# Decay-gate logits before the softmax attention, two value products in its last units, and GLA outputs with tokens on partitions

## The chip, the cores and the metric

The kernel runs on one core of a Trainium2 chip. The metric is the device time of one execution in microseconds (us), smaller is better. A comparison of this kernel with another can tell about 0.3% (some 3 us) from no change.

## The reference

One layer of a streaming encoder for 512 prompt tokens and 32 sample tokens (544 in all), D = 1024, all in float32. Cut to what the change touches:

```
h  = rmsnorm(x)
cq, ckv, kpe, gq, gk, gv, glr, gr, ga, gb = split(h @ w_in)
o_a = softmax attention over 8 heads (chunk causal)
la  = log_sigmoid(glr @ w_gate2 + b_gate2) / 16          # the decay gates, 4 heads x 128
o_g, state = gla(gq, gk, gv, la, state0)                 # 4 heads, keys 128, values 256 wide
o_b = rmsnorm(o_g over the 256 values of a head) * g_gla_norm * silu(gr)
x  += ( sigmoid(ga) * (o_a @ w_a) + sigmoid(gb) * (o_b @ w_b) ) @ w_out
x  += mixture of 32 experts, 2 of them per token;  y = rmsnorm(x)
```

## The kernel before, in words

Activations stand with features on partitions and the 544 tokens along the free dimension. A projection tile ("product", e.g. `("gv", 3)`) makes 128 features for all tokens: the weight tile is loaded (SyncE queue), its high part cast on ScalarE (`high`), its low part subtracted on GpSimd (`split`), and TensorE adds three terms (high x high, high x low, low x high) in 48 matmuls of 272 columns. Results go to one of two PSUM slots of `proj` in strict alternation; the list `outputs()` fixes the order, and `take(kind, j)` makes TensorE wait until the slot's last user has been read (`proj_read`). Everything on an engine runs in program order.

The order of the work on TensorE:

1. Norm and latents: cq, kv, kr products, then 15 groups of one-column matmuls that give the means for the latent norms (L1131, L1132), gr 0 to 3, the 8 query products `uq`, V and K.
2. Attention: 40 units (head pair, token tile, head). Unit u does its scores, then a third of a product from `ATT_FILL` (`fill_part`; in units 1 to 36), then the turn of unit u-2's probabilities, then every second unit the value product `pv`. DVE does maximum and normalisation, ScalarE the exponentials and PSUM copies.
3. When all 20 outputs of attention are split (`oa_done`): `gate_logits`, five matmuls of 512 columns into `bank`; DVE takes the minimum with 0, ScalarE Abs, Exp, Ln, DVE the difference `la`. TensorE meanwhile computes the products gv 0 to 7 and turns them (`turn_values`) so that `vtok` has tokens on partitions; `decays(0)` needs `la`.
4. GLA: chunks c = 0 to 4 (128 tokens; the last has 32). Per chunk TensorE does `decays(c+1)`, `chunk_scores(c)`, `turn_scores(c)`, product ga c, `og` (8 output blocks of 128 values x tokens, L1375 and, from chunk 1, L1377), product wa c, `new_values`. ScalarE per chunk: three PSUM copies, a dummy Exp that fetches the table, `exponentials(c+1)`, `chunk_gate` (Sigmoid), the copy of `og` into `gqk`. DVE per chunk, in this order: `masked(c)`, `new_state(c-1)`, `exponents(c+1)`, `gate_out(c)`, `decayed(c+1)`, `branch(0, c)`.
5. After chunk 4's scores: the norm of the outputs. The values are on partitions, so the mean square of each head is a matmul of the squares with a full matrix of 1/256 (`o_mean`, L1394, two matmuls of 512 columns per head), ScalarE takes the root, DVE the reciprocal over 128x512, GpSimd multiplies with the gates (`gate_output`), DVE with the norm. The last 32 tokens have 16 small matmuls of their own (`last_outputs`, L1402, L1403) and 8 for their means (L1421).
6. The rest of the branch products, wo, routing, and the 32 experts, whose weights (6 MB each) are streamed. The first expert load waits for product wb 7 and `mg_ready` 8.

Of the kernel before, what the change touches and what calls it, by code (L numbers as in the profile page):

```python
# [303 lines left out]
def _build(nc, t, ctx):  # L304
# [107 lines left out]
    gvT = [G(f"gvT{n}", [P, TOK]) for n in range(2)]  # L412
    vtok = G("vtok", [P, NT, GH * DV])
# [31 lines left out]
    osq = [D_(f"osq{n}", [P, 2, SEQ]) for n in range(2)]  # L445
    ors = [D_("ors0", [P, SEQ])]
    assert D_.at <= GS
    D_ = Region(MG0)
    ors.append(D_("ors1", [P, SEQ]))
    osq_d = D_("osq_d", [P, 2 * GH, DEC])  # L450
    ors_d = D_("ors_d", [P, GH, DEC])
    assert D_.at <= EXQ_AT
# [132 lines left out]
    gate_done = sem("gate_done")  # L585
# [147 lines left out]

    def output_part(h):
# [11 lines left out]
    def _(sp):  # L746
# [53 lines left out]
        for n in range(NRAW, len(WT)):  # L800
# [117 lines left out]
    def _(pool):  # L918
# [16 lines left out]
        def gate_output(h):  # L935

            pool.wait_ge(osq_ready, h + 1)
            part = output_part(h)
            nc.gpsimd.tensor_tensor(gqk[part], gqk[part], grs[part], ALU.mult).then_inc(og_gated, 1)

        gates_after = {("wa", 4): range(GH + 1)}
        low_outputs_after = {("wa", 5): range(EARLY_LOW)}
        for n in range(len(WT)):
            if n >= 2:
                split(n)
            for h in gates_after.get(WT[n], ()):
                gate_output(h)
# [70 lines left out]
    def _(pe):  # L1018
# [101 lines left out]
        product("kr", 0)  # L1120


        pe.wait_ge(consts_set, 1)
        pe.wait_ge(hTf_ready, NT)
        pe.wait_ge(proj_read[1], OUT_INDEX["cq", 1] // 2 + 1)
        pe.wait_ge(proj_read[0], OUT_INDEX["kv", 0] // 2 + 1)
        for i in range(NT):
# [4 lines left out]
            mm = pe.matmul(bank[0:r, 2, lat_col(1, i):lat_col(1, i) + 1], kvs[:, tok], mean128[:, 0:1], start=True, stop=True)  # L1132
# [28 lines left out]
        product("gr", 3)  # L1161
        pe.wait_ge(cqn_ready, 1)
# [86 lines left out]
        def gate_logits(c):  # L1249

            L = ROWS[c]
            pe.matmul(bank[0:L, c % 4, :], glr3[:, c * P:c * P + L], w_g3[:, :], start=True, stop=True).then_inc(gate_done, 1)

        for c in range(4):
            gate_logits(c)
        first = take("gv", 0)
        product_part("gv", 0, first, 0, 2)
        pe.wait_ge(gates_taken, 1)
        pe.wait_ge(gate_min, 1)
        gate_logits(4)  # L1260
# [1456 lines left out]
```

## Time and profile before

| | us |
|---|---|
| median of 3 runs | 1093.15 (1090.77 to 1093.94) |
| the profiled execution | 1090.68 |
| its span in the trace | 1088.9 |

| engine | busy share of the span |
|---|---|
| TensorE, matmul | 91% |
| DVE | 36% |
| ScalarE | 26% |
| GpSimd | 20% |

The 40 slices of the page show TensorE at 9 tenths through slice 22, some 600 us, with the DMA engines at 1 to 5 tenths; from slice 23 on the DMA engines are at 9 tenths at some 427 GB/s. A busy share is an average over both stages.

### The profile page before, as it was taken

What the parts mean: (1) busy time and instruction counts of PE and PEld (TensorE: products, weight loads), DVE (VectorE), ACT (ScalarE), POOL (GpSimd) and SP (SyncE); (2) the same over time, 40 slices, a digit from 0 to 9 for tenths busy, and PEclk for the clock granted to TensorE, in tenths of its full rate; (3) what the DMA queues carried; (4) which work ended last, traced back from release to release, by engine and by line L of the source; (5) the groups of instructions that cost most, each with busy time, mean ns of one, the idle gap of its engine ahead of it and who ended that gap; (6) DMA issues with size and microseconds to landing.
All of it is one profiled execution on the core that took longest, in us unless ns stands there. A gap on an engine that the chain in (4) does not pass through costs nothing.

```text
span 1088.9 us, 15322 instructions
## 1 busy us (share of the span) xinstructions
PE 995.8 (91%) x6337; PEld 687.5 (63%) x6337; DVE 396.2 (36%) x744; ACT 280.6 (26%) x456; POOL 219.1 (20%) x126
## 2 busy tenths in 40 slices
PE   8999999989999999999998999898887778888885
PEld 5996888879989799999996333333332333333332
DVE  7154843434776664312436122111111111111118
ACT  5436444473555361222215000000000000000012
POOL 0332122213312364343320111101101111010000
PEclk9999999999999999999999999988888889888898
DMA  9342521213121133433477999999999999999994
GB/s 225 90 91 78 181 58 44 59 38 89 50 59 30 49 117 80 143 112 98 173 301 275 410 429 425 426 426 425 428 427 428 426 427 427 429 426 427 423 415 165
DMA packets 108944, 267.58 MB, mean 246 GB/s; under 512 B 21821, under 2 KB 88797, under 8 KB 95666
## 3 DMA queue, kind: packets, MB, share of 16 engines
q1 hardware_dynamic: 104178, 258.06, 61.9%
q0 software_dynamic: 4704, 8.64, 2.1%
q8 instruction: 46, 0.75, 0.3%
q14 instruction: 16, 0.13, 0.0%
HBM read 256.12 MB, written 18.17 MB: 252 GB/s over the span
## 4 chain that ended last, share of the span: by engine, by line
PE 40%; DMA 24%; DVE 4%; issue 2%; ACT 2%; DVEq 0%; SPq 0%; ACTq 0%
DMA we<-in_w_exp_up 21%; PE proj L1071 18%; PE proj L1548 12%; DMA we<-in_w_exp_down 4%; PE proj L1564 4%; PE bank L1394 1%; DVE xsT L2575 1%; PE bank L1574 1%; PE bank L1444 1%; PE proj L1350 1%; ACT ex L1895 1%; DVE x_rows L2648 0%; DVE x_rows L2655 0%; PE proj L1550 0%; PE bank L1047 0%
## 5 line engine op out<-in xcount | busy, mean ns | idle before, releaser
L1548 PE MATMUL proj<-we,xsT 128*64 128x512 f32 x512 | 254.0, 654 | 63.0 <-DMA we<-in_w_exp_up 52.5
L1550 PE MATMUL proj<-we,xsT 128*64 128x512 f32 x512 | 254.3, 654 | 0.0
L925 POOL TENSOR_TENSOR wlo<-raw,whi 128x1024 fp32r<-128x1024 f32 x68 | 156.4, 2301 | 371.4 <-PE proj L1071 347.3
L1548 PEld LDWEIGHTS proj<-we,xsT 128*64 128x64 f32 x512 | 73.9, 150 | 210.5 <-issue 197.3
L1071 PE MATMUL proj<-hT_hi,whi 128*128 128x272 f32 x688 | 147.4, 296 | 0.6 <-ACT grs L1829 0.6
L1071 PE MATMUL proj<-hT_hi,wlo 128*128 128x272 f32 x688 | 145.7, 293 | 0.0
L1071 PE MATMUL proj<-hT_lo,whi 128*128 128x272 f32 x688 | 145.7, 293 | 0.0
L2567 DVE TENSOR_TENSOR hg<-hg,proj 64x512 f32<-64x512 f32 x32 | 22.1, 690 | 307.0 <-ACT hg L2067 293.5
L2067 ACT ACTIVATE hg<-proj 64x512 f32<-64x512 f32 x30 | 17.7, 590 | 421.7 <-PE proj L1550 421.7
L1564 PE MATMUL proj<-we,hT 128*64 128x512 f32 x256 | 115.2, 592 | 2.0 <-DVE hT L2570 1.1
L1565 PE MATMUL proj<-we,hT 128*64 128x512 f32 x256 | 115.2, 593 | 0.0
L1071 PEld LDWEIGHTS proj<-hT_hi,whi 128*128 128x128 f32 x688 | 109.3, 190 | 5.0 <-issue 1.9
L1071 PEld LDWEIGHTS proj<-hT_lo,whi 128*128 128x128 f32 x688 | 109.6, 190 | 3.1 <-issue 2.4
L1071 PEld LDWEIGHTS proj<-hT_hi,wlo 128*128 128x128 f32 x688 | 108.9, 190 | 2.8 <-issue 1.9
L963 POOL DMA_INDIRECT expert_out<-yo,sidx x30 | 29.8, 994 | 385.8 <-DVE sidx L2587 385.8
L1713 ACT CAST whi<-raw 128x1024 fp32r<-128x1024 f32 x70 | 69.8, 998 | 111.6 <-PE proj L1071 104.2
L1564 PEld LDWEIGHTS proj<-we,hT 128*64 128x64 f32 x256 | 34.8, 137 | 72.0 <-issue 70.8
L1550 PEld LDWEIGHTS proj<-we,xsT 128*64 128x64 f32 x512 | 74.0, 150 | 0.0
L2584 DVE COPY yo<-proj 128x512 f32<-128x512 f32 x30 | 20.8, 692 | 66.1 <-PE proj L1565 66.1
L2235 DVE TENSOR_REDUCE stat<-bank 128x1 f32<-128x128 f32 (+4 forms) x40 | 19.2, 480 | 43.0 <-PE bank L1194 42.9
L1565 PEld LDWEIGHTS proj<-we,hT 128*64 128x64 f32 x256 | 34.8, 137 | 0.0
L1194 PE MATMUL bank<-kcat,qT 100*128 100x128 f32 (+4 forms) x80 | 29.7, 455 | 1.1 <-ACT prob L1811 0.7
(369 smaller groups left out, 1398.2 us busy)
## 6 DMA issues: line engine op xcount, KB each, us to landing
we<-in_w_exp_gate SPq DMA_DIRECT2D x31, 2048.0 KB, 31.9
we<-in_w_exp_up SPq DMA_DIRECT2D x31, 2048.0 KB, 36.3
we<-in_w_exp_down SPq DMA_DIRECT2D x31, 2048.0 KB, 38.6
raw<-in_w_in SPq DMA_DIRECT2D x43, 512.0 KB, 3.9
x_rows<-in_x_prompt SPq DMA_DIRECT2D x8, 512.0 KB, 4.7
raw<-in_w_branch_b SPq DMA_DIRECT2D x8, 512.0 KB, 4.0
raw<-in_w_out SPq DMA_DIRECT2D x8, 512.0 KB, 4.1
zc<-expert_out SPq DMA_DIRECT2D x4, 1024.0 KB, 17.5
```

The lines of the kernel that those rows point to most:

```text
L925: nc.gpsimd.tensor_tensor(lo[:, 0:c], raw[n % NRAW][:, 0:c], hi[:, 0:c].bitcast(F32), ALU.subtract).then_inc(w_split, 1)
L963: pool.indirect_dma_start(out=ys[:, :], out_offset=bass.IndirectOffsetOnAxis(ap=sidx[s][:, 0:1], axis=0), in_=yo[:, s, :], in_offset=None, ...
L1071: mm = pe.matmul(proj[:, slot, half, 0:HALF], w[:, at:at + P], r[:, k, half * HALF:(half + 1) * HALF], start=(m == 0), stop=(m == len(term ...
L1194: pe.matmul(bank[0:r, u % 2, 0:n], qT[0:QK + TILES, h, q0:q0 + r], kcat[hp % 2][0:QK + TILES, a, k0:k0 + n], start=True, stop=True).then_i ...
L1548: pe.matmul(proj[0:SLOTS, s, 0, :], xsT[:, k, cols], wg[:, k * FF:(k + 1) * FF], start=(k == 0), stop=(k == KD - 1))
L1550: mm = pe.matmul(proj[64:64 + SLOTS, s, 0, :], xsT[:, k, cols], wu[:, k * FF:(k + 1) * FF], start=(k == 0), stop=(k == KD - 1))
L1564: pe.matmul(proj[0:SLOTS, s, 1, :], hT2[:, s, k, :], wd[:, k * D:k * D + FF], start=(k == 0), stop=(k == 3))
L1565: mm = pe.matmul(proj[64:64 + SLOTS, s, 1, :], hT2[:, s, k, :], wd[:, k * D + FF:(k + 1) * D], start=(k == 0), stop=(k == 3))
L1713: nc.scalar.copy(whi[n % NHIGH][:, 0:c], raw[n % NRAW][:, 0:c]).then_inc(w_high, 1)
L2235: v.tensor_reduce(stat[0:r, 1, u:u + 1], bank[0:r, u % 2, 0:n], AX.X, ALU.min).then_inc(negmax_ready, 1)
L2567: v.tensor_tensor(hg[0:SLOTS, s, :], hg[0:SLOTS, s, :], proj[64:64 + SLOTS, s, 0, :], ALU.mult).then_inc(done, 1)
L2584: v.tensor_copy(yo[:, s, :], proj[:, s, 1, :])
```

## The change

Four things are moved or redone.

- **Decay gates.** The five logit matmuls go to the place after product gr 3, ahead of `uq`. They take PSUM slots (four new entries `gl` in `outputs()`, the first holds two tiles), ScalarE copies them to SBUF (`gl`). The sizes (Abs) and Exp stand in attention units 23 to 26, 31 and 32, the minima on DVE in 24, 25, 32; Ln stands after unit 40's slot, before the late Silu.
- **Two value products.** gv 0 and gv 1 join `ATT_FILL`, so that units 37 to 42 have a third of a product too. After attention comes gv 2, and then the turns of gv 0 and gv 1.
- **GLA outputs** are computed with tokens on partitions. Per chunk four outputs of 256 columns; ScalarE copies them, squares each head with an accumulated sum along the free dimension, and takes the root; DVE the reciprocal of 128x4 and one multiplication over the chunk (`normed_output`, last in the chunk, ahead of the next `masked`). TensorE turns the normed chunk c-1 back (`turn_outputs`, 8 transposes into a PSUM slot, entry `ot`) after product ga c, DVE applies gain and gate from PSUM (`gated_chunk`). The `o_mean` matmuls, the 128x512 reciprocals and GpSimd's `gate_output` are gone.
- **The latent means** stand between the last five eighths of product kr and no longer after it.

```diff
+ATT_FILL += [("gv", j) for j in range(EARLY_GV)]          # EARLY_GV = 2
...
+SIZES_AT = {23: (0, 1), 24: (2, 3), 31: (4,)}
+EXPS_AT = {25: (0, 2), 26: (2, 4), 32: (4, 5)}
+MINIMA_AT = {24: (0, 1), 25: (2, 3), 32: (4,)}
...
+        if (k, j) == ("gr", EARLY_GR - 1):
+            o += [("gl", m, None) for m in range(len(GATE_TILES))]
...
-                o += fill[0:1] + ([("og", c, None)] if c < NT - 1 else []) + fill[1:]
+                o += fill[0:1] + ([("ot", c - 1, None)] if c else []) + ([("og", c, None)] if c < NT - 1 else []) + fill[1:]
...
+                sp.wait_ge(gate_min, 4)
...
-        gates_after = {("wa", 4): range(GH + 1)}
...
+        taken = take("kr", 0)
+        for part in range(8):
+            product_part("kr", 0, taken, part, 8)
...
+            if part >= 8 - NT:
+                mm = latent_means(part - (8 - NT))
...
         product("gr", 3)
+        pe.wait_ge(wg_split, 1)
+        for n, tiles in enumerate(GATE_TILES):
+            _, slot = take("gl", n)
+            for half, c in enumerate(tiles):
+                mm = pe.matmul(proj[0:ROWS[c], slot, half, :], glr3[:, c * P:c * P + ROWS[c]], w_g3[:, :], start=True, stop=True)
+            mm.then_inc(proj_done, 1)
...
-        for c in range(4):
-            gate_logits(c)
-        first = take("gv", 0)
...
+        product("gv", EARLY_GV)
+        for j in range(EARLY_GV):
+            turn_values(j)
...
+        def turn_outputs(c):
+            _, slot = take("ot", c)
+            pe.wait_ge(on_ready, c + 1)
+            for n in range(8):
+                mm = pe.transpose(proj[:, slot, n // 4, (n % 4) * P:(n % 4 + 1) * P], gqk[:, n, c * P:(c + 1) * P], ident)
+            mm.then_inc(proj_done, 1)
...
             if c:
                 product("ga", c)
+                turn_outputs(c - 1)
...
-            for n in range(8):
-                h = n // 2
+            for h in range(GH):
+                out = proj[0:L, slot, h // 2, (h % 2) * DV:(h % 2 + 1) * DV]
+                mm = pe.matmul(out, attT[0:L, h, 0:L], vtok[0:L, c, h * DV:(h + 1) * DV], start=True, stop=(c == 0))
                 if c:
-                    mm = pe.matmul(out, S_st[:, h, (n % 2) * P:(n % 2 + 1) * P], exQ1[:, h, :], start=False, stop=True)
+                    mm = pe.matmul(out, exQ1[:, h, :], S_st[:, h, :], start=False, stop=True)
...
-        o_mean(0)
         new_values(NT - 1)
-        o_mean(1)
...
-        last_outputs(0, 4)
-        o_mean(2)
-        o_mean(3)
-        last_outputs(4, 8).then_inc(last_og, 1)
+        for h in range(GH):
+            pe.matmul(bank[h * DEC:(h + 1) * DEC, 2, 0:DV], attT[0:DEC, h, 0:DEC], vtok[0:DEC, 4, h * DV:(h + 1) * DV],
+                      start=True, stop=False)
+        for h in range(GH):
+            mm = pe.matmul(bank[h * DEC:(h + 1) * DEC, 2, 0:DV], exQ1[:, h, :], S_smp[:, h, :], start=False, stop=True)
...
+            for h in range(GH):                               # ScalarE, after the copy of og
+                at = GH * c + h
+                step(nc.scalar.activation(o_junk[:, h, :, :], token_area(c)[:, 2 * h:2 * h + 2, :], ACT.Square,
+                                          scale=float(DV) ** -0.5, accum_out=o_stat[:, 0, at:at + 1]))
+            o_roots(slice(GH * c, GH * c + GH))
...
                 gate_out(c)
+                if c:
+                    gated_chunk(c - 1)
                 decayed(c + 1)
                 branch(0, c)
+                normed_output(c)
```

## Rows read from the trace of the kernel before

**Rows 1.** The page: mean busy share of the DMA engines in 40 slices.

```profile
DMA  9342521213121133433477999999999999999994
```

**Rows 2.** The page: the chain that ended last, by line.

```profile
DMA we<-in_w_exp_up 21%; PE proj L1071 18%; PE proj L1548 12%; DMA we<-in_w_exp_down 4%; PE proj L1564 4%; PE bank L1394 1%; DVE xsT L2575 1%; PE bank L1574 1%; PE bank L1444 1%; PE proj L1350 1%; ACT ex L1895 1%; DVE x_rows L2648 0%; DVE x_rows L2655 0%; PE proj L1550 0%; PE bank L1047 0%
```

**Rows 3.** Windows: stretch, length, busy us (count) per engine, PEclk, DMA share, GB/s.

```profile
42.33:45.27 2.94, 2.94 (x32) 2.91 (x30) 0.00 (x0) 2.72 (x4) 2.36 (x1) 1.00 0.00 0
45.27:52.91 7.64, 7.64 (x51) 7.64 (x49) 3.84 (x8) 1.68 (x5) 0.00 (x0) 0.78 0.41 69
...
219.55:230.31 10.76, 7.02 (x66) 4.23 (x64) 5.74 (x19) 5.63 (x16) 1.67 (x1) 1.00 0.20 51
...
319.57:338.10 18.53, 17.73 (x161) 16.75 (x161) 13.84 (x22) 11.04 (x13) 4.07 (x3) 1.00 0.17 44
...
358.62:386.05 27.43, 27.43 (x151) 20.37 (x149) 18.35 (x20) 13.03 (x18) 13.14 (x7) 0.94 0.17 49
```

**Rows 4.** Timeline, ScalarE at the end of gr 3: start us, us, what.

```profile
75.23 0.62 ACT L1759 ACTIVATE grs<-proj 128x544 f32<-128x544 f32 x1
```

**Rows 5.** Timeline, ScalarE's copy of a 128x512 PSUM result.

```profile
92.60 0.58 ACT L1789 COPY V<-proj 128x512 f32<-128x512 f32 x1 [0.27 <-PE proj L1171]
```

**Rows 6.** Windows of two us after the attention's end.

```profile
230.00:232.00 2.00, 1.69 (x4) 1.35 (x5) 1.22 (x4) 1.67 (x2) 0.00 (x0) 0.62 0.00 0
232.00:234.00 2.00, 2.00 (x10) 1.95 (x9) 1.49 (x3) 2.00 (x2) 0.00 (x0) 0.53 0.00 0
```

**Rows 7.** Timeline, TensorE: the gate logits, and the turn after gv 2.

```profile
230.31 1.94 PE L1252 MATMUL bank<-w_g,glr 96*128 96x512 f32 x4 [0.52 <-DVE oa_lo L2254]
...
251.71 0.60 PE L1284 MATMUL bank<-cst,gvT 128*128 128x128 f32 x4
```

**Rows 8.** Timeline, DVE in chunks 2 and 3.

```profile
323.59 0.69 DVE L2316 TENSOR_TENSOR att<-bank,cst 128x512 f32<-128x512 f32 x1 [1.46 <-issue]
...
339.94 0.71 DVE L2363 TENSOR_TENSOR msum<-proj,sg 128x544 f32<-128x544 f32 x1
342.23 0.69 DVE L2316 TENSOR_TENSOR att<-bank,cst 128x512 f32<-128x512 f32 x1 [1.57 <-issue]
```

**Rows 9.** Timeline, ScalarE in chunk 2.

```profile
331.22 2.77 ACT L1895 ACTIVATE ex<-ex 128x3072 f32<-128x3072 f32 x1 [4.10 <-issue]
...
334.62 1.28 ACT L1931 ACT_TABLE_LOAD   x1
335.92 0.66 ACT L1931 ACTIVATE sg<-sg 128x544 f32<-128x544 f32 x1
...
337.00 1.00 ACT L1962 COPY gqk<-proj 128x1024 f32<-128x1024 f32 x1
```

**Rows 10.** Timeline, ScalarE: an activation of 256 columns with an accumulated sum.

```profile
204.54 0.47 ACT L1811 ACTIVATE prob<-bank,stat 128x256 f32<-128x256 f32 x1 [0.81 <-DVE stat L2235]
...
204.91 0.19 ACT L1811 ACTIVATION_READ_ACCUMULATOR prob<-bank,stat 128x1 f32 x1
```

**Rows 11.** Timeline, TensorE: score matmuls on 32 columns each, then four transposes.

```profile
341.02 1.08 PE L1297 MATMUL bank<-ex 128*32 128x128 f32 x32
342.04 0.66 PE L1301 MATMUL bank<-cst,ex 128*128 128x128 f32 x4
```

**Rows 12.** Chain of waits in order of time: start us, us, what.

```profile
358.86 6.00 PE proj L1071 x48
...
368.92 1.91 PE bank L1394 x4
373.52 5.21 PE bank L1394 x8
381.42 3.10 PE proj L1071 x24
384.51 1.70 PE bank L1421 x16
```

**Rows 13.** Groups by line and shape: DVE over 1024 columns beside GpSimd, and alone.

```profile
L294 DVE TENSOR_TENSOR hT_lo<-hT_f,hT_hi 128x1024 fp32r<-128x1024 f32 x4 | 4.6, 1205 | 0.0
...
L2416 DVE TENSOR_TENSOR ob_lo<-gqk,ob_hi 128x1024 fp32r<-128x1024 f32 x2 | 4.6, 2314 | 0.0
```

More of the change, by code:

```diff
@@ L444, in _build @@
     D_ = Region(LA_AT)
[L445 to L452, printed above, removed]
+    o_junk = D_("o_junk", [P, GH, 2, P])
+    assert D_.at <= LA_AT + 2 * GH * DK * 4
     early_sums = [nc.alloc_sbuf_tensor_at(f"msum{n}", [P, TOK], F32, offset=at)
@@ L1119, in _, with latent_means @@
         product("kv", 0)
[L1120 to L1127, printed above, removed]
+        def latent_means(i):
             r = ROWS[i]
@@ L1781, in _ @@
             output_gate(j)
+        for n, tiles in enumerate(GATE_TILES):
+            o, _ = out_of("gl", n)
+            for half, c in enumerate(tiles):
+                last = nc.scalar.copy(gl[c][0:ROWS[c], :], proj[0:ROWS[c], o % 2, half, :])
+            last.then_inc(proj_read[o % 2], 1)
         for h in range(HEADS):
@@ L1838, in evict, with gate_sizes, gate_exps @@
                 nc.scalar.copy(halves(gqk[:, 4 + j, :]), ps).then_inc(proj_read[o % 2], 1)
+            if kind == "gv":
+                nc.scalar.copy(halves(gvT[j % 2][:, :]), ps).then_inc(proj_read[o % 2], 1)
+        def gate_sizes(tiles):
+            for c in tiles:
+                nc.scalar.activation(la[0:ROWS[c], c, :], gl[c][0:ROWS[c], :], ACT.Abs).then_inc(gates_taken, 1)
+        def gate_exps(a, b):
+            act.wait_ge(gates_taken, b)
+            step(nc.scalar.activation(la[0:ROWS[a], a:b, :], la[0:ROWS[a], a:b, :], ACT.Exp, scale=-1.0))
         NU = len(UNITS)
-        for u in range(NU + 2):
+        for u in range(NU + 3):
             if u < NU:
@@ L1858, in _ @@
         step(nc.scalar.activation(late, late, ACT.Silu))
-        for c in range(NT):
-            L = ROWS[c]
-            act.wait_ge(gate_min, c + 1)
-            nc.scalar.activation(la[0:L, c, :], bank[0:L, c % 4, :], ACT.Abs).then_inc(gates_taken, 1)
-        act.wait_ge(gates_taken, NT)
         def values(j):
@@ L1905, in copy_keys @@
             nc.scalar.copy(kdT[0:L, :, :], bank[0:L, 3, :].rearrange("p (h l) -> p h l", h=GH)).then_inc(kdT_copied, 1)
-        for j in range(1, 8):
+        for j in range(EARLY_GV, 8):
             values(j)
@@ L2370, in gate_out, with inverse_roots, normed_output, gated_output @@
             v.tensor_copy(halves(gate_home(0, c)[:, :]), ps).then_inc(proj_read[o % 2], 1)
+        def inverse_roots(c, cols):
+            dve.wait_ge(o_rms, c + 1)
+            v.reciprocal(o_stat[:, 2, cols], o_stat[:, 1, cols]).then_inc(o_inv, 1)
+            dve.wait_ge(o_inv, c + 1)
+        def normed_output(c):
+            inverse_roots(c, slice(GH * c, GH * c + GH))
+            area = token_area(c).rearrange("p (h n) l -> p h n l", n=2)
+            inv = o_stat[:, 2, GH * c:GH * c + GH].unsqueeze(2).unsqueeze(3).to_broadcast([P, GH, 2, P])
+            v.tensor_tensor(area, area, inv, ALU.mult).then_inc(on_ready, 1)
+        def gated_output(c, turned):
+            area = token_area(c).rearrange("p (h n) l -> p h n l", n=2)
+            gates = grs[:, :, c * P:c * P + ROWS[c]].rearrange("p (h n) l -> p h n l", n=2)
+            for n in range(2):
+                last = v.scalar_tensor_tensor(area[:, :, n, :], turned[n], g_gla[:, n:n + 1], gates[:, :, n, :], ALU.mult, ALU.mult)
+            last.then_inc(og_ready, 1)
+        def gated_chunk(c):
+            o, _ = out_of("ot", c)
+            turned = proj[:, o % 2, :, :].rearrange("p a (h n l) -> p (a h) n l", n=2, l=P)
+            gated_output(c, [turned[:, :, n, :] for n in range(2)])
+            dve.wait_ge(og_ready, c + 1)
+            dve.sem_inc(proj_read[o % 2], 1)
         for c in range(NT):
@@ L2416, in _ @@
             v.tensor_tensor(ob_lo[part], gqk[part], ob_hi[part].bitcast(F32), ALU.subtract).then_inc(ob_ready, 1)
+        dve.wait_ge(last_ot, 1)
+        gated_output(NT - 1, [bank[:, 1, n * P:(n + 1) * P].rearrange("p (h l) -> p h l", l=DEC) for n in range(2)])
+        dve.wait_ge(ob_ready, GH)
+        dve.wait_ge(ob_high, GH + 1)
+        part = output_part(GH)
+        v.tensor_tensor(ob_lo[part], gqk[part], ob_hi[part].bitcast(F32), ALU.subtract).then_inc(ob_ready, 1)
         branch(0, 5)
```

204 lines of the change are left out of this document (75 added, 129 removed).

## The prediction

> **What bounds the kernel now.** I read the page's slices first, then the chain of waits, then the windows of each stage, then single timelines. The slices show two stages [rows 1]: TensorE full and the DMA engines light for some 23 slices, then the DMA engines full. The chain says the same [rows 2]: projection matmuls (L1071), then expert weights. The first expert load waits for product wb 7, so the second stage starts when the first ends and has its own length, given by bandwidth. What TensorE saves ahead of the experts comes off the end in full, and what another engine saves there is worth nothing unless TensorE waits for it. So the sum is over TensorE's path in five places.
>
> **A. Latent means.** Now they take 2.94 us by themselves, and the product behind them takes 7.64 us at a granted clock of 0.78 [rows 3], where 48 such matmuls take 6.0 [rows 12]: the clock stood at 1.2 GHz for part of it and cost 1.6. After the change the same matmuls stand in pieces of 0.6 us between pieces of 0.75 us of full matmuls. They cost the same; the 1.6 goes if the clock holds. TensorE is then about half full over 7 us. Nearest row: the end of attention, 7.02 busy of 10.76 with small tiles [rows 3], which was followed by a fall [rows 6]. That is in between, so I take half: -0.8 (bounds -1.6 and +0.2, the latter since the DVE work behind kr starts 2.7 us later and its reciprocals come just as gr 0 ends).
>
> **B. Gate logits ahead of uq.** The first pair finds its slot free. The second needs gr 3's slot, and ScalarE first casts (1.05) and then does the Silu, until 75.85 [rows 4]; the cast starts 0.2 after TensorE is done with gr 3, so that is at 74.08 (75.23 - 0.95 - 0.2; casts and Silus overlap by 0.1). Then it copies 512 columns at some 0.52 us each behind one another (0.58 for one alone [rows 5]): gl 0 is two copies (76.9), gl 1 one, gl 2 one. The third logit slot waits for 76.9, the fourth for 77.45, and uq 0 for gl 2's copy, 78.1, plus signals: 78.2. So TensorE, with 1.1 us of matmuls, stands from 74.08 to 78.2: +4.1. A wait of 0.3 in uq 2, caused by ScalarE's same backlog, goes: -0.3. What is queued behind the wait is all of uq, V, K and attention; DVE idles there, so nothing hides it. Then the clock: two stretches of little TensorE work (the means in A; attention's end) were each followed by some 3.4 us at 1.2 GHz [rows 3, 6], and this gap is emptier than attention's end. At half clock 3.4 us lose 1.7. I take it: B = +5.5 (bounds +3.8 and +5.8).
>
> **C. End of attention.** From the scores of unit 37 to the logits 10.76 us pass, of which TensorE is busy 7.0; without the drain of last results its matmuls need 6.6, and the rest are waits for softmax steps and the last split [rows 3]. Then come logits (1.73 for four at 1.2 GHz, of their 1.94 with drain [rows 7], and 0.24 for the fifth) and gv 0, which loses 0.84 to the clock [rows 6]. gv 0, gv 1, gv 2 and two turns end at 252.2 (251.71 and a turn of 0.47 [rows 7]). New: 6.6 of attention matmuls, six parts of 2.0, the last wait 0.6, gv 2 6.0, two turns 0.9, total 26.2 from 219.55: 245.8. That is -6.4: idle 3.5, logits 2.0, clock 0.85. The Ln (table load 1.28, 1.92, 0.6) then stands at about 236 to 240, the late Silu to 245; `decays(0)` comes at 259, so `la` is 16 us early. In units 23 to 26 ScalarE gets 4 x 0.5 of Abs and 2 x 1.05 of Exp, some 4 us in 13 where it is half idle, and DVE 5 minima of 0.6 at most; probabilities are turned two units later, which covers it. Without that cover it costs up to 1. C = -6.4 (bounds -6.7 and -5). The new wait on SP (gate_min ahead of the state load) is met 40 us before.
>
> **D. Chunks.** `og` has the same columns (8 x 128 or 4 x 256) and the same time. Added on TensorE: 8 transposes of 128 columns, 4 of which take 0.43 back to back (their last ends 0.66 after the start, of which 0.2 is drain [rows 11]): 0.87 per chunk. TensorE's period is now 18.53 with 0.8 of waits [rows 3], so it would be 18.6. But `normed_output(c)` stands ahead of `masked(c+1)` on DVE, and behind it waits TensorE's `turn_scores` and the product ga. The loop from mask to mask: 323.59 to 331.22 for mask, state and exponents (7.6) [rows 8, 9]; exponentials to 334.6 (3.4) [rows 9]; then DVE needs 6.0 for `decayed` and `branch`, done at 340.65, with 1.57 to spare [rows 8]. ScalarE needs now 3.4 to the end of the `og` copy [rows 9]. New behind it: settle 0.15, four squares with their sum at 0.56 each (0.37 + 0.19 in sequence [rows 10]) = 2.25, settle 0.1, a table load for the root and the root 1.28 + 0.27 (a load and its follower stand 1.30 apart [rows 9]). That is 7.5 after the exponentials. DVE adds signal 0.1, reciprocal 0.15, one multiplication over 1024 columns 1.2 [rows 13], settle 0.1. Loop: 7.6 + 3.4 + 9.1 = 20.1 against 18.5 now. So the loop takes over from TensorE: the first mask +0.9 (there `branch` ended only 0.6 before it), the next two +1.6 each, and chunk 3 adds its transposes (0.87), less what waits absorb: D = +4.8. `gated_chunk` (two operations of 0.7) falls into the 2.9 us in which DVE waits for the exponentials. Lower bound: no loop, transposes less recovered waits, +1.3. Upper: DVE operations take up to twice as long beside GpSimd (2.31 for 1.2 [rows 13]), and a stalled chunk may lose clock: +10.
>
> The Trainium skill ("ScalarE: Activation LUTs", What ACT_TABLE_LOAD costs) gives 1.28 us for a load and 1.38 more for draining, 2.66 per switch; by that the loop would be 1.4 longer and D +9. The timeline shows the follower 1.30 after the load's start [rows 9], so the trace disagrees on the drain.
>
> **E. After the chunks.** From product ga 4 to product ga 5 pass 27.43 us [rows 3]. Removed: four `o_mean`, two of 1.91 each and two together in 5.21 with the clock low, the last outputs in the two gaps of 2.69 between these rows (370.83 to 373.52, 378.73 to 381.42), the small means 1.70 [rows 12]: 16.1. Added: turning chunk 3, 0.87, and the new last outputs, 8 matmuls of 256 columns into four groups of 32 partitions. No row has exactly these; nearest are the scores, 32 passes of 128 columns on 32 columns of the array in 1.02 [rows 11], so 16 passes of 256 take about 1.1. If they went one after another, 3.7 (16 passes at 0.23: an `o_mean` makes four passes of 512 columns in 1.91 [rows 12], and half the columns are half of that). I take 1.2, since both forms are 32 columns wide. Two transposes later: 0.3. E = -13.7 (bounds -14.0 and -11.1). What is late next: wb 0 needs all outputs split. ScalarE's four casts and the reciprocals that are gone leave them done some 6 us before wb 0, while DVE before had four reciprocals of 3.35 there. GpSimd loses its gate products, so its splits come no later.
>
> **Sum:** -0.8 + 5.5 - 6.4 + 4.8 - 13.7 = -10.6. Against the profiled execution (1090.68, span 1088.9) that is 1080.1. The median, 1093.15, lies 2.5 above that execution and would give 1082.5. I forecast 1081, between the two.
>
> **Rivals.**
> 1. *The chunk loop does not bind* (DVE gets its root in time). For: 1.57 to spare now. Against: the sum above overruns it by 1.6. D is +1.3: 1077.5. Chance 0.12.
> 2. *The last outputs run one after another*: the change would then not give there what its layout is for. For: all four groups of the first half read the same 32 rows. +2.5: 1083.5. Chance 0.13.
> 3. *The root's table switch costs twice*: the square after it or the root itself needs a second load in each chunk, 1.28 more [rows 9], three times: 1085. For: five functions alternate there. Against: squares and copies follow other tables without a load. Chance 0.07. By the Trainium skill's rule above it would be 1.38 each, the same time.
> 4. *Slower*: the mask-to-mask loop. Every microsecond that squares, root, norm or GpSimd's interference add there is paid three times, and it decides from 23.7 us per chunk (20.1 + 10.6/3) on. It needs DVE's 12 us per chunk to grow by a third, as if each second operation met GpSimd [rows 13]. At 25 us: 1096. Chance 0.04.
> 5. *Small gain*: the loop at 22 us and the clock low in A as well: 1088 to 1090. Chance 0.08.
>
> The forecast with its own spread (1078 to 1084) has 0.56. The range 1075 to 1088 takes in rivals 1 to 3 and most of the bounds of A to E; it leaves out rival 4 and 5. A measurement of this kernel tells about 0.3%, 3.3 us, from no change; faster by more 0.92, within it 0.04, slower 0.04.
>
> **What would show each step.** A: the clock in the product behind kr. B: a gap of some 4 us between gr 3 and uq 0, with waits for ScalarE's copies, and 1.2 GHz behind it. C: no TensorE gaps in units 37 to 42, the first value turn near 245 plus B. D: the start-to-start time of L2316 near 20 us, TensorE waiting before L1311 for DVE. E: ga 4 to ga 5 in some 13.5 us. The prediction is wrong if the chunks' period is far from 20, if the expert stage does not shift with its start, or if B's gap is hidden.

## The result and the profile after

The changed kernel takes 1080.9 us (median of 4 runs, 1078.04 to 1084.04) against 1093.55 for the kernel before, run beside it on the same chip: a ratio of 0.9885, 95% interval 0.9861 to 0.9910, so 12.6 us less. The profiled execution took 1079.51 us with a span of 1077.7, against 1090.68 and 1088.9. The forecast was 1081. The sum was nearly right, but each of its five terms was off, by 0.6 to 2.8 us, and the errors cancel: the closeness of the total is luck.

The page of the changed kernel, slices of the granted clock and of the DMA engines, and the chain by line [rows 1, 2]:

```profile
PEclk9999999999999999999999999999998999888898
DMA  9342432122121333433658999999999999999994
...
PE proj L1075 34%; DMA we<-in_w_exp_up 21%; PE proj L1533 12%; DMA we<-in_w_exp_down 4%; PE proj L1549 4%; PE bank L1210 2%; PE bank L1237 1%; PE bank L1223 1%; PE bank L1429 1%; DVE xsT L2586 1%; PE bank L1559 1%; PE proj L1187 1%; ACT ex L1890 1%; DVE x_rows L2666 0%; DVE hT_f L2127 0%
```

The two stages are as before: projection matmuls, now L1075, then expert weights.

The windows of the changed kernel that answer to [rows 3] (same columns); the third, new, is the gap ahead of uq 0, the fourth starts at the scores of unit 37, the last runs from product ga 4 to product ga 5:

```profile
38.95:45.24 6.29, 6.29 (x58) 6.13 (x56) 0.00 (x0) 0.17 (x1) 0.06 (x1) 1.00 0.33 83
45.24:51.35 6.11, 6.11 (x51) 6.07 (x49) 3.19 (x8) 4.14 (x8) 2.34 (x1) 1.00 0.38 73
72.55:76.55 4.00, 2.03 (x8) 0.70 (x6) 0.00 (x0) 3.70 (x7) 2.36 (x1) 1.00 0.07 7
221.67:230.31 8.64, 8.64 (x63) 6.73 (x62) 3.87 (x12) 4.27 (x10) 1.67 (x1) 1.00 0.24 63
...
321.64:340.94 19.30, 18.86 (x155) 17.04 (x153) 15.47 (x26) 13.79 (x23) 3.75 (x2) 1.00 0.17 47
358.31:373.16 14.85, 14.85 (x112) 13.34 (x109) 6.81 (x15) 7.24 (x12) 2.36 (x1) 0.89 0.53 160
```

Read from the top: the product behind the means now runs at full clock (6.11 us, before 7.64 at 0.78); 4.00 us between gr 3 and uq 0 hold 2.0 of matmuls; TensorE is full in the last units; a chunk is 19.3 long; and the last stretch is 14.85 long, before 27.43, at a clock of 0.89.

A table by stage says more than single rows, since a stage repeats from kernel to kernel where its code is the same and the clock did not fall: to 0.1 us in the middle columns, to some 0.6 in the first (54.83 to 55.45). The last column does not repeat (687.5 to 690.4, with low clocks in every execution that are not marked), so a difference of some 3 us between two totals can come from the experts alone; no run here shows what makes it. The marks are starts in the timelines: the first matmul on the low half of hT in cq 0, uq 0, the 512-column scores of unit 37, the masks of chunks 0 to 3, wb 0, the end. Each * is a stretch of some 3.4 us at 1.2 GHz within the stage (a "fall" from here on). All 14 kernels profiled (the 12 others are described below):

| kernel | cq 0 to uq 0 | to unit 37 | to mask 0 | mask to mask | to wb 0 | to the end |
|---|---|---|---|---|---|---|
| before | 52.56* | 145.47 | 66.39* | 19.54, 18.11, 18.64 | 58.95* | 687.7 |
| means_alone | 51.14 | 145.49 | 67.43** | 19.55, 18.11, 18.64 | 59.43 | 687.5 |
| gates_values_alone | 55.05 | 145.13 | 60.77 | 19.54, 18.11, 18.65 | 62.12** | 690.0 |
| gla_alone | 52.55* | 145.48 | 67.77** | 20.31, 18.88, 19.31 | 49.04* | 690.3 |
| **changed kernel** | 55.16 | 145.12 | 60.77 | 20.31, 18.89, 19.30 | 49.08* | 687.7 |
| no_values | 55.35 | 146.64* | 65.10* | 20.30, 18.89, 19.30 | 47.55 | 688.0 |
| norm_after_mask | 55.17 | 145.11 | 60.76 | 19.55, 23.50, 24.04 (**) | 47.57 | 689.2 |
| logits_hidden | 51.75 | 145.84 | 60.76 | 20.31, 18.89, 19.31 | 49.07* | 687.7 |
| low_on_dve | 55.17 | 146.57* | 60.76 | 20.31, 18.88, 19.32 | 47.83* | 687.7 |
| best | 52.12 | 145.84 | 60.76 | 19.54, 23.34, 23.94 (**) | 46.40 | 688.8 |
| squares_twice | 55.45 | 147.49** | 60.79 | 20.84, 20.61, 21.16 (*) | 49.06* | 690.4 |
| cast_late | 54.83 | 146.63* | 60.76 | 20.01, 18.64, 18.80 | 47.54 | 688.4 |
| hidden_low | 52.08 | 145.88 | 60.80 | 20.30, 18.88, 19.30 | 46.36 | 689.0 |
| three | 52.11 | 145.89 | 60.76 | 20.00, 18.66, 18.79 | 46.37 | 687.5 |

From before to the changed kernel: +2.60, -0.35, -5.62, +2.21, -9.87 and 0, with 0.1 at the start: 11.2, the difference of the two spans.

### The profile page after: what moved, and what is told of

Same layout as the page of the kernel before. It is cut to its first block, busy times and chain, and to the rows that moved or that the text cites. A ratio compares the mean times of both kernels' runs of the same rounds, so it can differ in the third digit from the quotient of the medians.

```text
span 1077.7 us, 15220 instructions
## 1 busy us (share of the span) xinstructions
PE 981.8 (91%) x6267; PEld 682.0 (63%) x6267; DVE 383.3 (36%) x752; ACT 286.1 (27%) x492; POOL 210.0 (19%) x121
## 4 chain that ended last, share of the span: by engine, by line
PE 61%; DMA 26%; DVE 6%; ACT 3%; issue 3%; POOL 1%; SPq 0%; DVEq 0%; ACTq 0%; POOLq 0%
PE proj L1075 34%; DMA we<-in_w_exp_up 21%; PE proj L1533 12%; DMA we<-in_w_exp_down 4%; PE proj L1549 4%; PE bank L1210 2%; PE bank L1237 1%; PE bank L1223 1%; PE bank L1429 1%; DVE xsT L2586 1%; PE bank L1559 1%; PE proj L1187 1%; ACT ex L1890 1%; DVE x_rows L2666 0%; DVE hT_f L2127 0%
## 5 line engine op out<-in xcount | busy, mean ns | idle before, releaser
L1533 PE MATMUL proj<-we,xsT 128*64 128x512 f32 x512 | 249.4, 644 | 67.5 <-DMA we<-in_w_exp_up 59.8
L1535 PE MATMUL proj<-we,xsT 128*64 128x512 f32 x512 | 249.8, 645 | 0.0
L1075 PE MATMUL proj<-hT_hi,whi 128*128 128x272 f32 x688 | 147.0, 295 | 2.5 <-POOL wlo L938 1.4
L1075 PE MATMUL proj<-hT_hi,wlo 128*128 128x272 f32 x688 | 145.2, 293 | 0.0
L1075 PE MATMUL proj<-hT_lo,whi 128*128 128x272 f32 x688 | 145.0, 292 | 0.0
L1075 PEld LDWEIGHTS proj<-hT_hi,whi 128*128 128x128 f32 x688 | 108.1, 188 | 7.4 <-issue 3.9
L1075 PEld LDWEIGHTS proj<-hT_lo,whi 128*128 128x128 f32 x688 | 108.5, 188 | 3.6 <-issue 2.8
L1075 PEld LDWEIGHTS proj<-hT_hi,wlo 128*128 128x128 f32 x688 | 108.1, 189 | 3.5 <-issue 2.5
L2353 DVE TENSOR_TENSOR mtmp<-proj,sg 128x544 f32<-128x544 f32 x8 | 5.8, 725 | 73.1 <-PE proj L1075 73.1
```

The source lines that it names most:

```text
L1075: mm = pe.matmul(proj[:, slot, half, 0:HALF], w[:, at:at + P], r[:, k, half * HALF:(half + 1) * HALF], start=(m == 0), stop=(m == len(term ...
L1533: pe.matmul(proj[0:SLOTS, s, 0, :], xsT[:, k, cols], wg[:, k * FF:(k + 1) * FF], start=(k == 0), stop=(k == KD - 1))
L1535: mm = pe.matmul(proj[64:64 + SLOTS, s, 0, :], xsT[:, k, cols], wu[:, k * FF:(k + 1) * FF], start=(k == 0), stop=(k == KD - 1))
```

## The experiments

**1. The parts alone.** Three kernels are the kernel before with one part of the change's diff each.

```diff
means_alone:
-        product("kr", 0)
+        for part in range(8):
+            product_part("kr", 0, taken, part, 8)
...
+                mm = latent_means(part - (8 - NT))

gates_values_alone:
+EARLY_GV = 2
+ATT_FILL += [("gv", j) for j in range(EARLY_GV)]
...
+            o += [("gl", m, None) for m in range(len(GATE_TILES))]
...
+            if u in SIZES_AT:
+                gate_sizes(SIZES_AT[u])

gla_alone:
+                out = proj[0:L, slot, h // 2, (h % 2) * DV:(h % 2 + 1) * DV]
+                mm = pe.matmul(out, attT[0:L, h, 0:L], vtok[0:L, c, h * DV:(h + 1) * DV], start=True, stop=(c == 0))
...
+                turn_outputs(c - 1)
...
+                normed_output(c)
```

> Only the latent means go between the sixteenths of kr 0; everything else as before. My theory (the stall at the means goes, and with it the clock fall behind it): the 512-column start of unit 37's scores comes 1.6 us earlier than in the kernel before (219.55) and the time is 1.6 us less. Rival (only the stall goes, the clock fall stays somewhere else): 0.8 us less.

> Only the gate logits ahead of uq 0 and the two value products in the attention's last units; latent means and GLA outputs as before. From the two traces the first costs 3.7 us up to unit 37 and the second gives 5.65 us back by the end of the second value turn: 2 us less than before in all. Rival (the parts help each other: without the new outputs the early vtok and decays only move a wait into the chunk loop): 0 us. Rival (what was lost to the clock at the end of attention comes back later): more than 4 us less.

> Only the GLA outputs with tokens on partitions; gate logits and means as before. From the two traces: chunk loop +3.2 us, stretch from the product ga 4 to the product ga 5 -12.6 us, the new wait for the split weights of gb 0 +1.4 us, together 8.0 us less than before. Rival (the parts are not additive, since the chunk loop is now entered with the DVE and ScalarE queues in another state): under 6 or over 10 us less, and then the masks of chunks 1 to 3 come at other distances than 18.9 and 19.3 us.

Measured: ratios to the kernel before of 0.9973 (0.9957 to 0.9989), 0.9980 (0.9959 to 1.0001) and 0.9898 (0.9875 to 0.9921), so -3.0, -2.2 and -11.2 us. They add up to -16 with an uncertainty of some 4, against -12.6 for all at once, so the times alone can't tell whether the parts add. The traces can: in the table each stage of the changed kernel is that of the kernel with its part alone (60.77 in gates_values_alone; 20.31, 18.88, 19.31 and 49.04 in gla_alone). No part needs another, and the rivals of interaction fall. gla_alone was expected at 8.0 less and its rival at over 10. The masks came at the distances expected (18.88 and 19.31), and up to wb 0 its traced chunks and their end give 7.7, so the rival's mechanism is not there; why the times give some 3 us more stays open.

The same rows show what spreading the means is worth. In gates_values_alone the means still stand in one block and the clock did not fall behind them: 55.05. The changed kernel, with the means spread, has 55.16. So spreading saves nothing that this column can show; its gain is the fall that it prevents: 52.56 to 51.14 from before to means_alone, 1.4 us. The block was followed by a fall in two of three executions (before, gla_alone), the spread form in none of eleven.

means_alone also shows something that the profile of before hides. TensorE there, behind the last small means:

```profile
386.58 0.52 PE L1071 MATMUL proj<-hT_hi,whi 128*128 128x272 f32 x2 [1.98 <-DVEq L2352]
```

The execution of before had a fall at 374 and no such wait; this one had the wait and no fall, and its stage is no shorter (59.43 and 58.95). The fall in before cost nothing, as VectorE was late behind it anyway. gates_values_alone has the same wait of 1.98, and a fall behind it, where nothing hides it: 62.12.

**2. No value products in the last units.**

```diff
-EARLY_GV = 2
+EARLY_GV = 0
```

> The changed kernel with no value product in the attention's last units (all eight behind them). My theory: the idle time of TensorE in the last units comes back and the two products with their waits stand behind it, while the gates' chain stays early: 4 to 5 us more than the changed kernel. Rival (the gain at the end of attention came from the gates' chain alone, which waited for nothing of the fill): within 1 us of the changed kernel. Rival (the idle time is as large as the two products, and was paid with a clock fall too): 8 us more.

Measured: 0.9918 (0.9902 to 0.9935), 3.6 us more than the changed kernel. From unit 37 to the first mask it takes 65.10 with a fall, before 66.39 with a fall, the changed kernel 60.77 with none. So the early gate chain gives 1.3 and the two products 4.3, inside the 4 to 5 expected (the 3.6 of the times is good to some 3 us, as is every difference of two such ratios below). The timeline of TensorE in no_values, waits at the end of attention:

```profile
226.30 0.63 PE L1223 MATMUL bank<-cst,prob 128*128 128x128 f32 x4 [1.25 <-ACT probT L1811]
...
230.04 0.31 PE L1223 MATMUL bank<-cst,prob 32*128 32x32 f32 x3 [0.86 <-DVE prob L2222]
231.90 0.31 PE L1223 MATMUL bank<-cst,prob 32*128 32x32 f32 x3 [0.53 <-ACT probT L1814]
232.57 0.66 PE L1237 MATMUL bank<-probT,V 128*64 128x32 f32 x12 [0.37 <-ACT probT L1814]
233.75 0.82 PE L1075 MATMUL proj<-hT_hi,whi 128*128 128x272 f32 x2 [0.52 <-DVE oa_lo L2233]
```

The changed kernel has only the last of them:

```profile
241.53 0.52 PE L1075 MATMUL proj<-hT_hi,whi 128*128 128x272 f32 x2 [0.52 <-DVE oa_lo L2233]
247.64 0.60 PE L1286 MATMUL bank<-cst,gvT 128*128 128x128 f32 x4
...
248.19 0.60 PE L1286 MATMUL bank<-cst,gvT 128*128 128x128 f32 x4
```

The matmuls behind the wait show the clock: the pair takes 0.82 in the first kernel and 0.52 in the second. The fall stands in all four executions without the products (before, means_alone, gla_alone, no_values) and in none of the ten with them.

**3. The gap ahead of uq 0.** TensorE in the changed kernel, between gr 3 and uq 0:

```profile
72.55 0.63 PE L1176 MATMUL proj<-w_g,glr 96*128 96x512 f32 x2
74.37 0.49 PE L1176 MATMUL proj<-w_g,glr 96*128 96x512 f32 x1 [1.19 <-ACT grs L1744]
75.33 0.91 PE L1176 MATMUL proj<-w_g,glr 96*128 96x512 f32 x2 [0.47 <-ACT gl L1770]
76.55 0.49 PE L1075 MATMUL proj<-cqn_hi,whi 128*128 128x272 f32 x2 [0.31 <-issue]
```

To take ScalarE's backlog away, logits_hidden takes the logits out of the alternating slots into a PSUM bank of their own and spreads them over gr 2 and gr 3:

```diff
+            pe.matmul(bank[0:ROWS[c], 3, :], glr3[:, c * P:c * P + ROWS[c]], w_g3[:, :], start=True, stop=True).then_inc(last_ot, 1)
...
+        pe.wait_ge(wg_split, 1)
+        for j in (2, 3):
+            taken = take("gr", j)
+            for part in range(2):
+                product_part("gr", j, taken, part, 2)
+                gate_logits(2 * j - 4 + part)
...
         for h in range(HEADS):
+            if h == 1:
+                gate_logits(4)
             product("uq", h)
```

> The gate logits of tiles 0 to 3 stand one at a time between the halves of gr 2, gr 3 and behind them, in a PSUM bank of their own, that of tile 4 behind uq 0; ScalarE copies each in between. My theory (the gap of 4.0 us ahead of uq 0 is ScalarE's backlog): the gap shrinks to 0.5 to 1 us, some 2.9 us less than the changed kernel, and where an execution of that has the lower clock behind the gap, 1.5 more. Rival (the logits' own time counts: the gap goes but each logit costs 0.6 us between full products): 1 to 1.5 us less. Rival (ScalarE's copies make its results of gr 2 and gr 3 late, and TensorE waits in uq 1 and uq 2): under 1 us.

Measured: 0.9849 (0.9834 to 0.9863), 1077.51 us, 3.9 us less than the changed kernel by the ratios. From cq 0 to unit 37 it takes 197.6 (198.0 in the three later kernels with the same logits) against 200.3 without a fall and 201.5 to 202.0 with one, so 2.3 to 2.7 of it are the gap. The rest fits the fall's share, but lies within the uncertainty of the times. TensorE there:

```profile
70.31 0.40 PE L1171 MATMUL bank<-w_g,glr 96*128 96x512 f32 x1
73.56 0.40 PE L1171 MATMUL bank<-w_g,glr 96*128 96x512 f32 x1
73.79 0.42 PE L1073 MATMUL proj<-cqn_hi,whi 128*128 128x272 f32 x2
```

uq 0 starts 0.23 behind the fourth logit; all five between full products cost 1.0 to 1.4 (197.6 to 198.0 against 196.6 in means_alone, which has none there). The theory holds, and the rivals of their price and of late results fall.

The clock behind the gap is the surprise. Seven kernels have the gap; the changed kernel's execution kept its clock behind it, as did two more (145.12, 145.13, 145.11 to unit 37), and four did not (146.64, 146.57, 146.63 and, with 6.8 us of it, 147.49). So the fall costs 1.5, or 2.4 at its longer form, and with the same code an execution has it or not. What decides it, no run here shows. The same TensorE rows in no_values, with 0.64 for the first pair where the changed kernel has 0.49:

```profile
76.35 0.64 PE L1075 MATMUL proj<-cqn_hi,whi 128*128 128x272 f32 x2 [0.32 <-issue]
76.79 0.66 PE L1075 MATMUL proj<-cqn_lo,whi 128*128 128x272 f32 x2
```

**4. The chunks' period.** Two experiments move the way from the outputs' copy to the next mask by a known amount, one up and one down.

```diff
squares_twice (ScalarE):
-            for h in range(GH):
+            for h in (*range(GH), *range(GH)):
...
+                if h == 0:
+                    step.settle()

cast_late (ScalarE):
-            if c < 4:
-                next_high(OUT[o][2])
...
             o_roots(slice(GH * c, GH * c + GH))
+            next_high(WT_INDEX["ga", c])
             out_of("wa", c)
```

> ScalarE takes each chunk's four squares with their sums twice (the second time behind the first; same results). They stand 0.40 us apart, so 1.6 to 1.8 us more of ScalarE per chunk. My theory (the way from ScalarE's copy of the outputs over squares, root and norm to the next mask sets the chunks' period): each of the three distances from mask to mask grows by the full 1.6 to 1.8 us, TensorE's waits ahead of turn_scores grow as much, and the time grows by 5 us against the changed kernel, or by more if a clock fall follows. Rival (the period is TensorE's own and its waits are chance): the waits take in part of it and the time grows by under 2 us.

> ScalarE's cast of the weights that follow ga c (0.60 us, it stands between the chunk's sigmoid and the copy of the outputs) goes behind the root. Nothing of the order on VectorE changes, and the work between a mask and the gate_out behind it neither. My theory: copy, squares and root come 0.5 to 0.6 us earlier, VectorE's waits for the root shrink from 1.96 and 1.73 us to about 1.3, the mask distances to 19.8, 18.5 and 18.7, TensorE's waits ahead of turn_scores from 1.04, 0.44, 0.77 to 0.5, 0 and 0.2: 1.5 us less than the changed kernel. Rival (the copy waits for TensorE's outputs anyway): under 0.5 us less. Rival, as in the run with the norm behind the mask (an operation of VectorE falls beside GpSimd's split): 2 us or more longer.

Measured: squares_twice 0.9911 (0.9876 to 0.9945), 2.8 us more than the changed kernel, wide; its mask distances are 0.53, 1.72 and 1.86 longer, 4.1 together. cast_late 0.9869 (0.9844 to 0.9894), 1.7 us less, of which its trace shows 1.05 in the distances: 0.30, 0.25, 0.50. By the times alone neither is clear of the changed kernel; the verdict rests on the distances. TensorE's waits ahead of `turn_scores`, first in squares_twice, then in cast_late (changed kernel: 1.04, 0.44 and 0.74; the expectations have 0.77 for the last):

```profile
307.18 0.66 PE L1313 MATMUL bank<-cst,att 128*128 128x128 f32 x4 [1.56 <-DVE att L2308]
327.79 0.66 PE L1313 MATMUL bank<-cst,att 128*128 128x128 f32 x4 [2.17 <-DVE att L2308]
348.95 0.66 PE L1313 MATMUL bank<-cst,att 128*128 128x128 f32 x4 [1.08 <-DVE att L2308]
```

```profile
304.20 0.66 PE L1313 MATMUL bank<-cst,att 128*128 128x128 f32 x4 [1.26 <-DVE att L2305]
322.86 0.66 PE L1313 MATMUL bank<-cst,att 128*128 128x128 f32 x4 [0.23 <-DVE att L2305]
341.65 0.66 PE L1313 MATMUL bank<-cst,att 128*128 128x128 f32 x4 [0.23 <-DVE att L2305]
```

The third wait of squares_twice grew by only 0.34, because a fall behind the mask had made TensorE itself later; the mask still waited for the root, VectorE by 2.48. VectorE's wait in the changed kernel, at the same place:

```profile
339.59 0.18 DVE L2365 RECIPROCAL o_stat<-o_stat 128x4 f32<-128x4 f32 x1 [1.96 <-ACT o_stat L1933]
```

For the second and third distance a microsecond on that way is a microsecond of time, until it is some 0.3 to 0.5 shorter than now; there the mask waits for TensorE's scores, and the time goes by TensorE's 18.6 to 18.8. The first distance is another case: ahead of mask 1 VectorE was itself the last (its wait for the root is zero there), so only 0.53 of the added 1.7 appears.

norm_after_mask then tried to take the root out of the way altogether:

```diff
             if c:
                 masked(c)
             if c:
+                normed_output(c - 1)
                 new_state(c - 1)
...
                 branch(0, c)
-                normed_output(c)
```

> In each chunk VectorE multiplies the outputs by the inverse root only behind the next chunk's mask. My theory (VectorE's wait for the root, 1.96 and 1.73 us, and the 1.4 us of the multiplication stand ahead of the mask and set the period): the masks come 18.5 to 18.7 us apart instead of 20.3, 18.9 and 19.3, TensorE's waits ahead of turn_scores (1.04, 0.44, 0.77) go, the first output of ga 4 comes 1.5 to 2 us earlier and the time is as much less. Rival (the period is TensorE's own, with the transposes added): the masks stay at 18.9 and 19.3, gain under 0.5 us. Rival (what is put behind the mask delays the state and the exponentials by 1.4 us, and the loop stays as long): no gain or up to 1 us more.

Measured: 0.9963 (0.9949 to 0.9977), 8.5 us more than the changed kernel. The third rival had the direction, none the size. VectorE, GpSimd and TensorE in chunk 2:

```profile
332.29 1.23 DVE L2281 TENSOR_SCALAR ex<-ex 128x2048 f32<-128x2048 f32 x1
333.43 2.84 DVE L2282 TENSOR_TENSOR ex<-bS 128x512 f32<-128x512 f32 x1
336.19 0.68 DVE L2283 TENSOR_TENSOR ex<-bS 128x512 f32<-128x512 f32 x1
```

```profile
333.36 2.36 POOL L938 TENSOR_TENSOR wlo<-raw,whi 128x1024 fp32r<-128x1024 f32 x1 [9.89 <-PE proj L1075]
```

```profile
333.05 1.03 PE L1361 MATMUL proj<-cst,gqk 128*128 128x128 f32 x8
337.56 0.89 PE L1386 MATMUL proj<-vtok,attT 128*128 128x256 f32 x2 [3.48 <-DVE sg L2360]
```

The matmuls of `og` need the PSUM slot of the product ga c, which VectorE empties behind the exponents (L2360). In the changed kernel that copy ends 8.2 us behind the start of the mask, at 329.83, and `og` starts at 329.88, so it has next to no slack:

```profile
329.11 0.72 DVE L2360 COPY sg<-proj 128x544 f32<-128x544 f32 x1
329.88 0.70 PE L1386 MATMUL proj<-vtok,attT 128*128 128x256 f32 x2
```
The norm put 1.34 in front of it, and this pushed an operation of 0.68 beside GpSimd's split, where it took 2.84. The copy came 3.5 later, TensorE waited 3.48, and at the emptied place the clock fell for 3.4 us (`og` in 5.06 instead of 3.37). 3.48 + 1.69, less the 0.46 by which the wait ahead of `turn_scores` is shorter, is 4.7, the difference of the distances (24.04 and 19.30). Chunk 1 repeats it with a wait of 3.04, and the kernel named best, which has this edit too, shows 23.34 and 23.94.

**5. The end of GLA.** In the changed kernel GpSimd and then TensorE:

```profile
373.47 1.30 POOL L938 TENSOR_TENSOR wlo<-raw,whi 128x512 fp32r<-128x512 f32 x1 [6.40 <-PE proj L1075]
374.73 5.75 POOL L946 TENSOR_TENSOR ob_lo<-gqk,ob_hi 128x1024 fp32r<-128x1024 f32 x2
380.44 5.88 POOL L938 TENSOR_TENSOR wlo<-raw,whi 128x1024 fp32r<-128x1024 f32 x2
```

```profile
383.93 0.49 PE L1075 MATMUL proj<-hT_hi,whi 128*128 128x272 f32 x2 [1.37 <-POOL wlo L938]
```

```diff
-EARLY_LOW = 2
+EARLY_LOW = 1
```

> One of the two low halves of the outputs goes from GpSimd to VectorE. My theory (two subtractions of 2.9 us on GpSimd make the split of gb 0 late): TensorE's wait of 1.37 us ahead of gb 0 goes; ob_lo on VectorE still ends ahead of wb 0; 1.4 us less than the changed kernel. Rival (the next wait moves in its place, since VectorE is then late for wb 0 or wa 5): within 0.5 us of the changed kernel.

Measured: 0.9868 (0.9853 to 0.9883), 1.9 us less than the changed kernel, but the two intervals overlap. The trace is clearer: the wait is 0.20, and from mask 3 to wb 0 it takes 47.83 against 49.08, both with a fall. The wait's cause is shown; of its 1.37 us 1.2 are won.

```profile
384.31 0.49 PE L1075 MATMUL proj<-hT_hi,whi 128*128 128x272 f32 x2 [0.20 <-POOL wlo L938]
```

**6. Together.** best is norm_after_mask, logits_hidden and low_on_dve at once. hidden_low leaves the norm where it was, and three adds the later cast to hidden_low.

```
best:        logits_hidden + (EARLY_LOW = 1) + norm_after_mask
hidden_low:  logits_hidden + (EARLY_LOW = 1)
three:       logits_hidden + (EARLY_LOW = 1) + cast_late
```

> The three edits of the runs beside it at once: the norm behind the mask, the logits between the halves of gr 2 and gr 3, one low half moved to VectorE. If each theory holds and they add, 1.7 + 2.9 + 1.4 = 6 us less than the changed kernel: a ratio to the kernel before of 0.983. If only the logits hold: 3 us less, 0.9858.

> The logits between the halves of gr 2 and gr 3, and one low half of the outputs moved from GpSimd to VectorE. By the traces of the two single runs the first gives 3.4 us from the start to the scores of unit 37 (4.9 where the clock falls behind the gap) and the second 1.4 us ahead of gb 0: 4.8 us less than the changed kernel, a ratio to the kernel before of 0.984. Rival (the second gives nothing, as its median was 1 us off the changed kernel): 0.985 or more.

> The two edits of the run beside it and the later cast in each chunk. If the three add: 4.8 + 1.5 = 6.3 us less than the changed kernel, 0.9827 of the kernel before. If the later cast gives nothing, the same as the run beside it.

Measured: best 0.9898 (0.9883 to 0.9914), as the norm gives back what the others gain. hidden_low 0.9839 (0.9816 to 0.9862), 1076.13 us. three 0.9827 (0.9803 to 0.9851), 1074.61 us, 6.3 us less than the changed kernel, as expected, and the fastest of all. Its execution had no fall at all ahead of the experts.

## Why the prediction was right, and where not

| term | forecast | shown by the two traces | error |
|---|---|---|---|
| A. means | -0.8 | -1.4 | -0.6 |
| B. gap | +5.5 | +4.0 - 0.35 = +3.7 | -1.8 |
| C. end of attention | -6.4 | -5.6 | +0.8 |
| D. chunks | +4.8 | +2.2 + 1.0 = +3.2 | -1.6 |
| E. behind them | -13.7 | -12.6 + 1.7 = -10.9 | +2.8 |
| sum | -10.6 | -11.0 | -0.4 |

(A is from before to means_alone, B from the gap's window and the next column. D's second number is from mask 3 to ga 4, 16.39 to 17.37; E's are ga 4 to ga 5, and ga 5 to wb 0, 15.13 to 16.86.) B and E lie just outside their own bounds (+3.8, -11.1), and the sum hides it.

**A.** Right in kind: the means cost the same, and the gain is the clock's. I took half of it for want of a near row. The nearest row I used (the end of attention, with a fall) was not near: there TensorE stood idle for a third of the time, while here 58 matmuls fill all of 6.29 us. A busy share alone does not explain it either: the block of before was busy for all of its 2.94 us, and the fall came behind it. Why the spread form keeps the clock stays open.

**B.** The gap was forecast as 4.1 and is 4.0, wait by wait (Silu, copy, signal). The 1.7 for the clock was added as certain. Where the fall comes it costs 1.5 to 2.4, as forecast; it comes in four of seven executions. A term with a chance belonged into the range, not whole into the sum.

**C.** Right in mechanism (idle, logits and clock all gone), 0.8 off in size. The stretch to the end of the second turn is 27.0 instead of 26.2, with the last wait at 0.52 where 0.6 was counted. Its matmuls, 26.46 busy, less 12.0 for the parts, 6.1 for gv 2 and 1.0 for the turns leave 7.3 for attention's own, where I had 6.6. I had taken a drain of last results off the busy time; among full products it did not go. That reading is only argued.

**D.** The mechanism holds (experiment 4): the way over ScalarE and VectorE sets the second and third distance. The size was the step "four squares with their sum at 0.56 each": 0.37 and 0.19 are not in sequence. ScalarE in the changed kernel:

```profile
336.17 0.42 ACT L1958 ACTIVATE o_junk<-gqk 128x256 f32<-128x256 f32 x1
336.49 0.19 ACT L1958 ACTIVATION_READ_ACCUMULATOR o_junk<-gqk 128x1 f32 x1
336.59 0.40 ACT L1958 ACTIVATE o_junk<-gqk 128x256 f32<-128x256 f32 x1
...
337.90 1.28 ACT L1933 ACT_TABLE_LOAD   x1
339.19 0.30 ACT L1933 ACTIVATE o_stat<-o_stat,eps_col 128x4 f32<-128x4 f32 x1
```

The next square starts 0.1 behind the start of the reading, so four take 1.7, not 2.25. The rest of chunk 2 came as worked out: mask to exponentials 7.64 (7.6), exponentials 3.4, the way to the next mask 8.26 (9.1), together 19.3 for 20.1. In chunk 1 the first part is only 7.21, since its state is one copy of 1.22 where chunk 2 has four operations of 1.65; the sum gave both chunks the longer form, before and after. So the loop binds by only 0.3 to 0.5 over TensorE's own 18.6.

**E.** The outputs in four groups of 32 partitions took 1.14 (forecast 1.2), the removed work was as listed:

```profile
364.40 1.03 PE L1361 MATMUL proj<-cst,gqk 128*128 128x128 f32 x8
...
367.39 0.63 PE L1397 MATMUL bank<-vtok,attT 32*32 32x256 f32 x8
367.96 0.64 PE L1400 MATMUL bank<-S_smp,exq 128*32 128x256 f32 x8
```

Two things were missed. "GpSimd loses its gate products, so its splits come no later" is wrong. GpSimd in the kernel before, behind the product ga 5 that started at 386.05 (in the changed kernel, shown in experiment 5, ga 5 starts at 373.16):

```profile
386.64 4.75 POOL L933 TENSOR_TENSOR ob_lo<-gqk,ob_hi 128x1024 fp32r<-128x1024 f32 x2
392.47 2.41 POOL L925 TENSOR_TENSOR wlo<-raw,whi 128x1024 fp32r<-128x1024 f32 x1 [1.08 <-PE proj L1071]
```

Its low halves started 0.59 behind ga 5 and now start 1.57 behind it: the split ahead of them waits for the end of wa 4, and the small means that stood between wa 4 and ga 5 are gone. They now take 5.75 for 4.75 and the split of gb 0 3.34 for 2.41, beside VectorE's own low halves (375.46 to 381.56). Before, that split ended 0.28 ahead of gb 0; now TensorE waits 1.37 for it. And a fall of the clock in wa 4, behind the last outputs, costs 1.5 (49.08, and 47.55 in kernels alike in this stage but for it). It came in five of the eleven executions with the new outputs, so it too is a term with a chance. In before a fall in this stage was free, as VectorE was late behind it.

**The rivals.** 1 (the loop does not bind): refuted by squares_twice for two of three distances, though the size, 3.2, lies halfway between its 1.3 and the 4.8 of the sum. 2 (outputs one after another): refuted, 1.14. 3 (the table switch costs twice): each chunk has one load ahead of the root, 1.28, and the root starts 1.29 to 1.30 behind its start (337.90 and 339.19 above). The Trainium skill ("ScalarE: Activation LUTs", What ACT_TABLE_LOAD costs) counts a further 1.38 for draining; the trace disagrees here as it did before the change. 4 (slower by the loop): not here, but norm_after_mask reached 23.5 and 24.0, where I had put the break-even at 23.7 for all three distances. Of its 3.5 us of delay 2.2 are the mechanism named, an operation beside GpSimd, and 1.3 the norm itself; with the first distance at 19.55 it kept 4 us of the gain. 5 (small gain): not here.

## What to carry to other kernels

Before an operation moves on an in-order engine, list what it pushes: behind the mask stood a PSUM release with no slack and an operation just clear of GpSimd, and 1.34 us in front of them cost 4.6 and 4.7 us in two chunks, while taking a cast of 0.6 out of the way was safe. Where the engine that bounds the kernel runs thin, give it whole products from later on, for the time and for the clock. Compare stages between marks over several kernels and not only totals: the stages ahead of the experts repeat to 0.1 us in the middle ones, while the four times of the changed kernel alone lie 6 us apart.

## What the runs showed of the hardware

- The clock behind a thin stretch is not a property of the code alone. Behind the same 4.0 us gap it fell in four of seven executions, behind the means in two of three, behind the unfilled end of attention in four of four, behind the last outputs in five of eleven. One fall of 3.4 us costs 1.5 us of full products, or nothing if TensorE waits later anyway.
- The last outputs, 16 matmuls of 256 columns, each on 32 columns of the array, took 1.14, against 3.37 for the 16 of an `og` on the full array: four groups of columns ran side by side, also where all four read the same 32 rows.
- An activation with an accumulated sum costs 0.40 from one to the next at 256 columns; the reading of the sum is mostly hidden.
- A VectorE operation of 0.68 took 2.84 beside a GpSimd split of 2.36. It ended at 336.27, 0.55 behind GpSimd's 335.72, as if it had stood still beside it. The copy of 0.72 that reads PSUM (329.11) and the two operations behind it (1.41) ran beside a split of 2.38 at 329.19 in the changed kernel and were not longer.
